# Attention front of a two-block transformer kernel: x and first tile loaded by halves in turn, angles on GpSimd, function tables loaded elsewhere, query tile's low part by two engines

## The reference, cut to what matters

```python
h = x @ w_in
c_q, k, v, k_idx, w_idx = jnp.split(h, ...)        # 256, 128, 128, 128, 8 columns
c_q = rms_norm(c_q, g_cq)
q = (c_q @ w_uq)...                                # query
q_idx = (c_q @ w_iq)...                            # index query, 8 heads of 128
k_idx = layer_norm(k_idx, g_ik, b_ik)
q_idx = apply_rope(q_idx, cos_i, sin_i); k_idx = apply_rope(k_idx, cos_i, sin_i)
rel = relu(einsum('bqhd,bsd->bhqs', q_idx, k_idx)) # scores by which 64 keys are chosen
score = einsum('bqh,bhqs->bqs', w_idx, rel); _, sel = lax.top_k(score, 64)
```

## Time and profile before

| | us |
|---|---|
| median of 3 runs | 1054.96 (1054.44 to 1059.04) |
| profiled execution, its own time | 1054.04 |
| its span, first to last instruction | 1052.2 |
| PE busy in the span | 1030.8 (98%) |
| chain of work that ended last, share by engine | PE 93%, DVE 3%, ACT 2%, DMA 1% |
| granted TensorE clock, mean | 0.998 |

### The profile page before, as it was taken

One profiled execution on the slowest core, in us unless ns is written; L12 is line 12 of the kernel. 1 busy time (PEld: TensorE's weight loads), 2 busy tenths in 40 slices (PEclk: granted clock), 3 DMA queues, 4 the chain that ended last, 5 costly groups with the idle time before them and its releaser, 6 DMA issues.

```text
span 1052.2 us, 17961 instructions
## 1 busy us (share of the span) xinstructions
PE 1030.8 (98%) x7744; PEld 953.1 (91%) x7744; DVE 469.6 (45%) x761; ACT 562.2 (53%) x787; POOL 783.5 (74%) x218
## 2 busy tenths in 40 slices
PE   7989999999999998999999999999999999999997
PEld 7868899998889997899998899999999988999986
DVE  4874253349825786427322152921263242533303
ACT  6684544443358785454444356466568446444420
POOL 4826798879678733789888768777774968988880
PEclk9999999999999999999999999999999999999999
DMA  9405555555545331675555346554442655555541
GB/s 358 157 2 180 220 201 196 183 190 193 199 176 185 128 129 67 227 255 186 198 197 200 123 184 230 184 186 142 177 178 102 220 185 195 200 197 187 186 153 40
DMA packets 27454, 186.59 MB, mean 177 GB/s; under 512 B 3168, under 2 KB 3424, under 8 KB 5872
## 3 DMA queue, kind: packets, MB, share of 16 engines
q1 hardware_dynamic: 25184, 178.83, 47.1%
q10 hardware_dynamic: 2192, 6.62, 1.9%
HBM read 184.39 MB, written 1.05 MB: 176 GB/s over the span
## 4 chain that ended last, share of the span: by engine, by line
PE 93%; DVE 3%; ACT 2%; DMA 1%; POOL 0%; issue 0%; DVEq 0%; SPq 0%; POOLq 0%; ACTq 0%
PE ps L410 29%; PE ps L412 28%; PE ps L411 28%; ACT arena L875 1%; PE ps L1528 1%; PE ps L1200 1%; DMA stage<-in_tiles 1%; PE ps L2242 0%; ACT arena L884 0%; PE ps L761 0%; DVE arena L1088 0%; PE ps L2247 0%; DVE ps L1804 0%; PE ps L1547 0%; DVE arena L1785 0%
## 5 line engine op out<-in xcount | busy, mean ns | idle before, releaser
L394 POOL TENSOR_TENSOR wl<-stage,wh 128x2048 fp32r<-128x2048 f32 x165 | 762.6, 4645 | 232.7 <-ACT wh L390 212.7
L390 ACT ACTIVATE wh<-stage 128x2048 fp32r<-128x2048 f32 (+1 forms) x167 | 317.8, 1907 | 117.7 <-DMA stage<-in_tiles 116.9
L410 PE MATMUL ps<-xh,wh 128*128 128x256 f32 x1328 | 369.7, 278 | 1.1 <-DVE wl L537 1.1
L411 PE MATMUL ps<-xl,wh 128*128 128x256 f32 x1328 | 368.0, 277 | 0.0
L412 PE MATMUL ps<-xh,wl 128*128 128x256 f32 x1328 | 368.0, 277 | 0.0
L410 PEld LDWEIGHTS ps<-xh,wh 128*128 128x128 f32 x1328 | 249.6, 188 | 3.5 <-issue 1.5
L411 PEld LDWEIGHTS ps<-xl,wh 128*128 128x128 f32 x1328 | 250.1, 188 | 0.1
L412 PEld LDWEIGHTS ps<-xh,wl 128*128 128x128 f32 x1328 | 249.3, 188 | 0.0
L410 PE MATMUL ps<-wh,xh 128*128 128x512 f32 (+2 forms) x400 | 134.5, 336 | 1.1 <-DVE xl L1137 0.9
L412 PE MATMUL ps<-wh,xl 128*128 128x512 f32 (+2 forms) x400 | 132.6, 331 | 0.0
L411 PE MATMUL ps<-wl,xh 128*128 128x512 f32 (+2 forms) x400 | 132.4, 331 | 0.0
(11 more groups left out here) (379 smaller groups left out, 1138.0 us busy)
## 6 DMA issues: line engine op xcount, KB each, us to landing
stage<-in_tiles SPq DMA_DIRECT2D x167, 1024.0 KB, 4.9
arena<-in_ln_g ACTq DMA_DIRECT2D x4, 512.0 KB, 3.8
arena<-in_ln_b ACTq DMA_DIRECT2D x4, 512.0 KB, 5.2
arena<-in_x_t SPq DMA_DIRECT2D x1, 1024.0 KB, 5.3
x_res<-in_x SPq DMA_DIRECT2D x1, 1024.0 KB, 21.4
out<-x_res SPq DMA_DIRECT2D x4, 256.0 KB, 2.0
stage<-in_tiles SPq DMA_DIRECT2D x1, 544.0 KB, 9.6
arena<-in_pre_mix_norm ACTq DMA_DIRECT2D x1, 512.0 KB, 6.8
```

What stands on the lines that cost most here:

```text
L390: nc.scalar.activation(tile_of(wh, n, *part), tile_of(stage, n, *part), ACT.Copy).then_inc(hi_done, 1)
L394: nc.gpsimd.tensor_tensor(tile_of(wl, n), tile_of(stage, n), tile_of(wh, n).bitcast(F32), ALU.subtract).then_inc(lo_done, 1)
L410: mm(out_, lh, rh, start=start, stop=False, skip_group_check=skip)
L411: mm(out_, lh, rl, start=False, stop=False, skip_group_check=skip)
```

## The change: what it does

1. SP issues x and tile 0 as halves in turn (x first half, tile 0 first half, x second half, tile 0 second half), then tile 1, then `cst`, then tile 2 and on. ACT and DVE split and subtract in the same order.
2. ACT issues positions and 24 frequency columns (`freq`) as DMAs of its own; the whole of `cst` moves to SP's queue.
3. The angles are worked out by POOL (`angles_pool`) between its set-up and its first low part. DVE no longer does them. [...]
4. ACT loads the table that holds Sin first, runs Sin behind tile 0's last quarter and ahead of tile 1, and loads the logarithm and exponential table behind tile 1. Three table loads become two.
5. The squares of c_q go ahead of tile 3 on ACT, and their sums ahead of the last two k blocks of tile 1's product on PE.
6. The low part of tile 2: POOL writes columns 0 to 511 and 1024 to 1535, DVE the other half (`iq_lo`).
7. Tile 5's high part is written in two halves (`hi_half`) between steps of the index query.
8. The warm-up is six identity products in place of twelve.

The core of the diff:

```diff
-            nc.scalar.dma_start(cst[:], A["consts"]).then_inc(c_in, 16)
+            nc.scalar.dma_start(freq, A["consts"][:, 302:326]).then_inc(freq_in, 16)
...
+        def angles_pool(pool):
...
+            f24 = tmp[:, 0, 0:2]
+            x, n = ang24, turns24[:, 4, :]
+            pool.wait_ge(pos_in, 16)
+            step_pool(gp.tensor_copy(f24, pos_i))
+            pool.wait_ge(freq_in, 16)
+            for c in range(2):
+                for t in range(2):
+                    last = gp.tensor_scalar(x[:, c * 48 + t * 24:c * 48 + (t + 1) * 24], freq, f24[:, t:t + 1], None, ALU.mult)
+            step_pool(last)
+            for c in range(2):
+                cols = slice(c * 48, (c + 1) * 48)
+                last = gp.tensor_scalar(n[:, cols], x[:, cols], 1 / (2 * math.pi), 0.0 if c else 0.25, ALU.mult, ALU.add)
+            step_pool(last)
+            step_pool(gp.tensor_scalar(n, n, MAGIC, None, ALU.add))
+            step_pool(gp.tensor_scalar(n, n, MAGIC, None, ALU.subtract))
+            for i, part in enumerate(TURN):
+                last = gp.tensor_scalar(turns24[:, i, :], n, -part, None, ALU.mult)
+            step_pool(last)
+            for i in range(len(TURN)):
+                step_pool(gp.tensor_tensor(x, turns24[:, i, :], x, ALU.add))
+            step_pool(gp.tensor_scalar(x[:, 0:48], x[:, 0:48], math.pi / 2, None, ALU.add))
+            gp.tensor_scalar(x, x, 3.1415925, -3.1415925, ALU.min, ALU.max).then_inc(reduced.sem, reduced.up())
...
         def setup_x_act(act):
+            setup_loads(act)
+            nc.scalar.preload_act_table_set("trig_and_small")
+            for h in range(2):
+                act.wait_ge(xt_in[h], 16)
+                for c in range(2 * h, 2 * h + 2):
+                    nc.scalar.activation(two(xh, c), two(x_raw, c), ACT.Copy).then_inc(xh_done.sem, xh_done.up())
+                act.wait_ge(stage_in[0] if h else w0_in, 16)
...
+            setup_act2(act)
+            hi_until(act, 1)
             nc.scalar.preload_act_table_set("natural_log_exp_and_others")
...
             pe.wait_ge(consts.sem, consts.due(pe, 2))
-            keep_warm(7, 12)
+            keep_warm(7, 6)
...
+                    if t == 1 and k == 5:
+                        pe.wait_ge(cq_ready.sem, cq_ready.due(pe))
+                        pe.wait_ge(sq_done.sem, sq_done.due(pe))
+                        squares_summed()
...
+                    if n == 2 and c:
+                        pe.wait_ge(iq_lo.sem, 1)
...
             index_plain(1)
+            hi_half(5, 0)
             index_turned(1)
+            hi_half(5, 1)
...
+            dve.wait_ge(hi_done, 3)
+            for a in (512, D + 512):
+                c = (a, a + 512)
+                last = V.tensor_tensor(tile_of(wl, 2, *c), tile_of(stage, 2, *c), tile_of(wh, 2, *c).bitcast(F32), ALU.subtract)
+            last.then_inc(iq_lo.sem, iq_lo.up())
...
-            sp.dma_start(x_raw, A["x_t"]).then_inc(xt_in, 16)
-            for n in range(RING):
+            for h in range(2):
+                ks, cols = slice(4 * h, 4 * h + 4), (h * TW // 2, (h + 1) * TW // 2)
+                sp.dma_start(x_raw[:, ks, :], A["x_t"][:, ks, :]).then_inc(xt_in[h], 16)
+                sp.dma_start(tile_of(stage, 0, *cols), A["tiles"][0, :, cols[0]:cols[1]]
+                ).then_inc(stage_in[0] if h else w0_in, 16)
+            load(sp, 1)
+            sp.dma_start(cst[:], A["consts"]).then_inc(c_in, 16)
+            for n in range(2, RING):
                 load(sp, n)
...
             setup_pool(pool)
-            for n in range(2, 6):
+            angles_pool(pool)
+            lo_part(pool, 2, (0, 512))
+            lo_part(pool, 2, (D, D + 512)).then_inc(lo_done, 1)
+            for n in range(3, 6):
                 lo(pool, n)
```

More of the change, by code:

```diff
@@ L314, in build @@
         late_in = sem("late_in")
-        xt_in = sem("xt_in")
+        xt_in = [sem(f"xt_in{h}") for h in range(2)]
+        w0_in, freq_in = sem("w0_in"), sem("freq_in")
         stage_in = [sem(f"stage_in{s}") for s in range(RING)]
@@ L508, in setup_act2 @@
             nc.scalar.activation(trig[:, :, :, :].rearrange("p c t f -> p (c t f)"),
-                                 ang24.rearrange("p c f -> p (c f)"), ACT.Sin).then_inc(trig_done.sem, trig_done.up())
+                                 ang24, ACT.Sin).then_inc(trig_done.sem, trig_done.up())
         TURN = []
@@ L521, in step, with step_pool, lo_part @@
             dve.wait_ge(dve_step.sem, dve_step.now())
+        def angles_pool(pool):
+            gp = nc.gpsimd
+            def step_pool(ins):
+                ins.then_inc(pool_step.sem, pool_step.up())
+                pool.wait_ge(pool_step.sem, pool_step.now())
+            f24 = tmp[:, 0, 0:2]
[20 more added lines that the diff above has]
+            gp.tensor_scalar(x, x, 3.1415925, -3.1415925, ALU.min, ALU.max).then_inc(reduced.sem, reduced.up())
+            pool.wait_ge(reduced.sem, reduced.now())
+        def lo_part(pool, n, c):
+            pool.wait_ge(hi_done, n + 1)
+            return nc.gpsimd.tensor_tensor(tile_of(wl, n, *c), tile_of(stage, n, *c), tile_of(wh, n, *c).bitcast(F32), ALU.subtract)
         def reduce_angles(dve, x, n, y, width):
@@ L540, in setup_dve @@
         def setup_dve(dve):
[L541 to L548, removed]
+            for h in range(2):
+                for c in range(2 * h, 2 * h + 2):
+                    x_lo(dve, c, x_raw)
+                for c in range(2 * h, 2 * h + 2):
+                    if c < 3:
+                        dve.wait_ge(first_hi.sem, c + 1)
+                    else:
+                        dve.wait_ge(hi_done, 1)
+                    first_low(0, (c * QUARTER, (c + 1) * QUARTER))
             dve.wait_ge(hi_done, 2)
             first_low(1, (0, KD * IW))
[L551 to L560, removed]
         def setup_dve2(dve):
@@ L623, in setup_x_act @@
         def setup_x_act(act):
-            nc.scalar.preload_act_table_set("natural_log_exp_and_others")
[L625 to L636, removed]
+            setup_loads(act)
+            nc.scalar.preload_act_table_set("trig_and_small")
+            for h in range(2):
+                act.wait_ge(xt_in[h], 16)
+                for c in range(2 * h, 2 * h + 2):
+                    nc.scalar.activation(two(xh, c), two(x_raw, c), ACT.Copy).then_inc(xh_done.sem, xh_done.up())
+                act.wait_ge(stage_in[0] if h else w0_in, 16)
+                for c in range(2 * h, 2 * h + 2):
+                    part = (c * QUARTER, (c + 1) * QUARTER)
+                    ins = nc.scalar.activation(tile_of(wh, 0, *part), tile_of(stage, 0, *part), ACT.Copy)
+                    if c < 3:
+                        ins.then_inc(first_hi.sem, first_hi.up())
+                    else:
+                        ins.then_inc(hi_done, 1)
+            setup_act2(act)
+            hi_until(act, 1)
+            nc.scalar.preload_act_table_set("natural_log_exp_and_others")
         def x_lo(dve, c, src):
@@ L704, in dsa_pe, with squares_summed @@
             last.then_inc(used, 1)
+            def squares_summed():
+                for t in range(2):
+                    for k in range(2):
+                        last = mm(ps[:, 3, t:t + 1], cqt[:, k, t * P:(t + 1) * P], mean_hd[:, 0:1], start=k == 0, stop=k == 1)
+                last.then_inc(ss_ps.sem, ss_ps.up())
             low_ready(pe, 1)
@@ L740, in keys_part @@
                 return last
[L742 to L747, removed]
             query(2, 1, (6, 7)).then_inc(iq_ps.sem, iq_ps.up())
@@ L947, in dsa_act @@
             last.then_inc(sq_done.sem, sq_done.up())
-            setup_act2(act)
-            nc.scalar.preload_act_table_set("natural_log_exp_and_others")
+            hi_until(act, 3)
+            late_loads(act)
             act.wait_ge(ki_var.sem, ki_var.due(act))
@@ L961, in dsa_act, with hi_half @@
             act.wait_ge(rs_cq.sem, rs_cq.now())
-            hi_until(act, 5)
+            hi_until(act, 4)
+            def hi_half(n, h):
+                act.wait_ge(stage_in[ring(n)], come[n])
+                part = (h * TW // 2, (h + 1) * TW // 2)
+                ins = nc.scalar.activation(tile_of(wh, n, *part), tile_of(stage, n, *part), ACT.Copy)
+                if h:
+                    ins.then_inc(hi_done, 1)
+                    his[0] += 1
             def index_plain(t):
```

8 lines of the change are left out of this document (3 added, 5 removed).

## The result

The changed kernel takes **1065.58 us** (median of 4 runs, 1065.16 to 1066.52) against 1054.72 for the kernel before: ratio 1.0099, 95% interval 1.0084 to 1.0113. It is 10.9 us slower, about 1.0% and clear of the 0.5%, 10 us from the forecast and outside its range. The profiled execution has a span of 1063.4, 11.2 over before.

What follows compares the result with a forecast made beforehand. TensorE bounds the kernel (busy 961.8 of 973 us from 80 us), so front shifts count whole. S +0.4, normalisation +0.1, tile 2 +0.1 gave +0.6: 1054.6 in the profiled execution's terms, 1055.6 against the median; range 1052.3 to 1058.8.

Steps and rivals of the forecast that it cites:

- A shift of the front: From 80 us to the end PE is nearly always busy, so any shift before that reaches the end whole.
- S: Start of tile 1's product on PE, the comparison mark: 16.40 us before the change, predicted 16.8.
- R + 2.9: S as R plus Sin 0.28, tile 1's high part 1.10, low part 1.29 and four hand-overs at 0.06.
- R: End of POOL's angles: frequencies at 6.3, plus 4.6 for POOL's instructions, plus 3.0 of waiting for DVE, 13.9 us.
- POOL's wait for VectorE: POOL's angle instructions and DVE's two-input SBUF subtractions exclude each other, costing POOL 3.0 us, at most 3.7.
- What I had counted behind S: Delays after tile 1's product starts: index key normalisation 0.1 us and tile 2's low part 0.1 us.
- Landing of the frequencies: Small position and frequency packets pass about twice as fast between 4 KB ones, landing at 6.3 us, bounds 5.0 to 9.6.
- POOL's instructions: POOL's nineteen angle instructions, with POOL's waits on itself, take 4.6 us, bounds 4.0 to 6.9.
- POOL's small instructions are dear: Rival, chance 0.12: POOL's angles at the two-input price, 6.9 us, inputs at 7.3; R = 17.2, S = 20.1, time 1058.8.
- the mechanism to which I gave 0.04: Rival: frequencies land at 9.6 and POOL's chain takes twice 4.6; R = 18.8, S = 21.7, time 1060.4; chance 0.04.
- a rival with 0.05: Clock falls again after PE idles before tile 1; half of tile 1's 5.3 us at double price, +2.6, 1058.2; chance 0.05.
- the start: PE's first product at 7.3 us at half speed, clock rise at 10.4, tile 0's product ending at 14.4.

Runs made afterwards that it cites:

- fill18: Changed kernel with eighteen identity products added on TensorE between tile 0's product and the wait for tile 1: 1060.80 us, ratio 1.0048.
- small_late: sin_late with the DMAs of positions and frequencies issued only behind x's first landing: 1057.56 us, ratio 1.0021.
- alone: Changed kernel with POOL's angles held back until VectorE has written the last low quarter of tile 0: 1069.51 us, one execution.
- w12_late: sin_late with twelve identity products at the start in place of six: 1057.06 us, ratio 1.0014.
- fill: Changed kernel with twelve identity products added on TensorE between tile 0's product and the wait for tile 1: 1059.98 us, ratio 1.0062.
- warm12: Changed kernel with twelve identity products at the start again: 1066.07 us, ratio 1.0116.
- sin_late: Changed kernel with Sin and its table loads moved back behind tile 3's high part on ScalarE, angles still on POOL: 1056.61 us, ratio 1.0018.
- dve_ang: w12_late with the angles back on VectorE behind tile 1's low part and the frequencies' own DMA gone: 1053.77 us, ratio 0.9981.

## Why the prediction was wrong, point by point

**What held.** A shift of the front reaches the end whole: 11.3 us at the transposes, 11.2 in the span. The path to S is right: POOL's angles, Sin, tile 1's high and low part; R + 2.9 came out as 18.5 + 2.7 = 21.2. The products started at the 1.2 GHz level behind the short warm-up. POOL's wait for VectorE is there: I had put 3.0 us, it measured 2.4, all of it on POOL's side. What I had counted behind S, 0.2 us for normalisation and tile 2, is best read in fill18, where the clock stays up: from S to the transposes 34.03 − 21.80 = 12.2 us, before 28.43 − 16.40 = 12.0.

**The step that failed first: R, the end of POOL's angles, 13.9 predicted and 18.5 measured.** Two of its three terms were too small, and the third (3.0 for 2.4) a little too large.
- *Landing of the frequencies, 6.3 estimated, 8.4 measured (+2.1).* I took it that small packets pass twice as fast between packets of half the size. The queues of 3 to 5 us, first of the kernel before, then of the changed one (packets, MB, share of 16 engines):

```profile
q1 hardware_dynamic: 98, 0.78, 99.0%
q10 hardware_dynamic: 97, 0.00, 2.7%
```

```profile
q1 hardware_dynamic: 89, 0.31, 62.0%
q10 hardware_dynamic: 96, 0.00, 2.4%
```

The number of packets stayed nearly the same, about one of each queue in turn; what fell was the bytes. So the small ones came no sooner and the large ones later than I had estimated: x's first half at 5.7 instead of 4.4, tile 0's at 8.0 instead of 5.9. With no small packets in the stretch, small_late moved 0.43 MB in it, so they explain a part; why 4 KB packets alone stay below 0.78 I haven't found out.
- *POOL's instructions, 4.6 us estimated, 7.7 alone (+3.1).* I priced TENSOR_SCALAR by AFFINE_SELECT and MEMSET, 0.22 at 96 columns and 0.12 at 24. Alone, six of the seven with 96 columns take 0.45 us (the last one 0.27), and those with 24 columns 0.35. The 0.45 is more than the two-input TENSOR_TENSOR at 96 columns, 0.39, which I had taken as the upper bound of a price. So the 7.7 lies outside the bounds that I gave, 4.0 to 6.9. The rival "POOL's small instructions are dear" carried 0.12 and gave R = 17.2 and 1058.8; it comes nearer. Nearest is the mechanism to which I gave 0.04, R = 18.8 and 1060.4, but by luck: it has the frequencies at 9.6, where they landed by 8.4, and a chain of 9.2, where it took 10.1.

The groups of the changed kernel, 8 to 19 us (busy us, mean ns), where the first is beside VectorE and the others are not, and last the first group in alone:

```profile
L539 POOL TENSOR_SCALAR arena<-arena 128x24 f32<-128x24 f32 x4 | 3.1, 788 | 2.1 <-DMA arena<-in_consts 2.1
L548 POOL TENSOR_SCALAR arena<-arena 128x96 f32<-128x96 f32 x4 | 1.8, 449 | 0.3
L551 POOL TENSOR_TENSOR arena<-arena 128x96 f32<-128x96 f32 x4 | 1.6, 392 | 0.3
...
L540 POOL TENSOR_SCALAR arena<-arena 128x24 f32<-128x24 f32 x4 | 1.3, 346 | 6.5 <-DVE wl L575 6.5
```

The Trainium skill (GPSIMD Engine Reference, Engine selection) calls GpSimd about twice as slow as VectorE with two inputs and "roughly line-rate" with one. For one input at this size the traces do not agree, and the measurement decides: a TENSOR_SCALAR of 96 columns takes 0.45 us on GpSimd, and 0.27 on VectorE in the kernel before (line 529, in PSUM). The Trainium skill's rule on the shared port (SBUF — State Buffer, Who interferes with whom) says that GpSimd's reads and a VectorE instruction with two SBUF inputs lock each other out. What these traces show of it is the one direction: 788 ns beside VectorE's subtractions against 346 alone, while the subtractions grew by 0.07 us a pair at most. VectorE's side of it stands in the 4.876 us of the earlier trace rows alone.

With R as measured and the clock up, S is 4.8 us late, and the time 1054.7 + 4.8 = 1059.5: 0.7 above the upper end of my range.

**The step that failed second: the clock.** I had it as a rival with 0.05, for half of tile 1's 5.3 us, +2.6. By the mean clock (0.987 to 0.990) it fell in all four executions of the changed kernel, and in the profiled one not for 2.6 us of work but for 13.7 us of time, across tile 1, the sums and half of the query. It cost 5.3 to 6.0 us by the times, 6.5 by the marks. I had reasoned from a wait of 1.08 us that does no harm, while my own case had one of 2.4. The trace of the kernel before has longer ones near 400 us, which I had not set against it: two waits of 2.0 and 2.1 us, and in the second of them the clock fell, for 3.4 us (timeline of PE, then the stretch):

```profile
396.50 0.49 PE L1559 MATMUL ps<-arena 128*128 128x128 f32 x2 [2.00 <-ACT arena L1680]
399.94 0.80 PE L1559 MATMUL ps<-arena 128*128 128x128 f32 x2 [2.07 <-ACT arena L1680]
```

```profile
399.60:402.90 3.30, 2.96 (x32) 2.74 (x34) 3.09 (x3) 1.49 (x8) 0.00 (x0) 0.50 0.00 0
```

In the front, the profiled executions have falls beside idle times of 1.3, 1.7, 2.2, 2.7, 3.0, 4.6, 5.9 and 6.1 us, and none where the longest idle time behind the first product was 1.1 us or less. More than that isn't settled: in the changed kernel the clock fell 1.3 us after PE had begun again, in w12_late 0.3 us after it had stopped, and in four executions of fill it did not fall for so long or not at all, so the length of the last idle time alone does not decide it. The failed R and the fall hang together: had R been 13.9, tile 1 would have been ready at 16.8, before tile 0 ended at 18.2, and there would have been no wait in front of it.

**A third, smaller: the start.** Products at 9.5 instead of 7.3, and the rise of the clock at 15.7 instead of 10.4, so tile 0 ended at 18.2 and not at 14.4. That the rise would stay where it was behind half the warm-up was assumed; with twelve products again (warm12) it came at 8.9. In the changed kernel all this is hidden behind R; in sin_late it is 1.2 us at S.

**Which part of the change did what.** Sin ahead of tile 1 made POOL's angles the path: about 9 us with its fall of the clock. The angles on POOL cost 3.3 us even without that. Six identity products in place of twelve put S 2.3 us later (17.61 in sin_late, 15.34 in w12_late), but there the time did not follow, since PE waited at the query instead. The loads by halves brought 0.9 us at S, and by the traces the halves of tile 5 kept most of it. The early squares and the split of tile 2 were not undone one by one. The version without the first three is dve_ang, 0.2% faster than before.

## What to carry to other kernels

Before a small chain of work goes to an engine that is idle, count what stands behind its consumer in that consumer's queue, and price each instruction by one of its own kind; if the trace has none, the dearer neighbour is no upper bound, and the chain should be placed so that it may be twice as long. Idle time of TensorE ahead of dense work is to be priced with the clock's fall, here 5.3 to 6.0 us for 3.0 us of idleness. Look in the whole trace of the kernel before for waits of that length and for what the clock did beside them. Products of the identity can fill the time, where they leave no more than about a us of it. When a transfer is cut in halves, look at what else shares its engines in packets.

## What the runs showed of the hardware that was not expected

- After a fall TensorE stayed at 1.2 GHz for 13.7 us though it was busy all the time (13.60 of 13.60 us), in other kernels for 3.4 or 6.8 us, and for 17.1 and 20.5 us behind idle times of 5.9 and 6.1 (warm12, alone).
- The same program has the long fall in one execution and not in the next: fill in one of five by the mean clock, which moves its time by 6 us. Near 400 us, beside the waits of 2 us there, the profile of every kernel has a short fall, of 3.4 us in before and warm12 and of 6.8 in the others.
- A wait for the shared port can be one-sided: four GpSimd instructions of 0.35 us took 0.79 each beside VectorE's two-input subtractions, whose pairs took 1.29 to 1.36 us instead of 1.29.
- Two DMA queues took turns packet by packet. Beside some 97 small packets in 2 us, 98 large ones moved 0.78 MB; when the large ones were of half the size, 89 of them moved 0.31 MB.
- A GpSimd TENSOR_SCALAR of 24 columns takes 0.35 us, one of 96 columns 0.45 (one of seven 0.27), a TENSOR_TENSOR of 96 columns 0.39.
